# Attention scores: the low-key products of two PSUM banks on 64 rows each, ahead of the full-row products

## What is computed

```
def mla_attend(q_n, q_r, k_n, k_r, v):
    s = jnp.einsum('bqhd,bkhd->bhqk', q_n, k_n) + jnp.einsum('bqhr,bkr->bhqk', q_r, k_r)
    p = jax.nn.softmax(s.astype(jnp.float32) * MLA_SCALE, axis=-1)
    return jnp.einsum('bhqk,bkhd->bqhd', p.astype(v.dtype), v)
...
    qn_l, qr_l = q_side(s_lat)
    qr_l = apply_rope(qr_l, cos[:, None, :], sin[:, None, :])
    kn_all = jnp.concatenate([kn_c, kn_l], axis=1)
    kr_all = jnp.concatenate([kr_c, kr_l], axis=1)
```

## Time and profile before

| | |
|---|---|
| median of 3 runs | 3030.64 us (3027.17 to 3031.13) |
| the profiled execution's own time | 3030.1 us |
| its span in the trace | 3028.3 us |
| TensorE busy, of the span | 2884.8 us (95%) |
| VectorE, ScalarE, GpSimd busy | 51%, 39%, 8% |
| granted TensorE clock, mean | 0.978 of 2.4 GHz |

### The profile page before, as it was taken

One profiled execution on the slowest core, in us unless ns is written; L12 is line 12 of the kernel. 1 busy time (PEld: TensorE's weight loads), 2 busy tenths in 40 slices (PEclk: granted clock), 3 DMA queues, 4 the chain that ended last, 5 costly groups with the idle time before them and its releaser, 6 DMA issues. The chain is left out here.

```text
span 3028.3 us, 38367 instructions
## 1 busy us (share of the span) xinstructions
PE 2884.8 (95%) x15527; PEld 2468.4 (82%) x15527; DVE 1531.3 (51%) x2792; ACT 1190.3 (39%) x1980; POOL 249.6 (8%) x291
## 2 busy tenths in 40 slices
PE   6999999999999999979979997999999999999798
PEld 4788888888888888868867886888888888887587
DVE  6536543554355535543333224666666666665444
ACT  5323312331233123332234213666666666665400
POOL 2100000000000000001220000202102022020000
PEclk9899999999999999989989998999999999999899
DMA  6301131113111311153341321001000101000522
GB/s 190 104 23 53 44 109 31 52 44 108 31 52 44 111 31 50 34 211 119 119 146 39 98 91 39 29 25 32 26 25 26 36 18 33 29 22 18 191 84 84
DMA packets 220177, 200.77 MB, mean 66 GB/s; under 512 B 12037, under 2 KB 190613, under 8 KB 220002
## 3 DMA queue, kind: packets, MB, share of 16 engines
q1 hardware_dynamic: 204946, 176.52, 19.0%
q0 software_dynamic: 4656, 16.56, 1.4%
q10 hardware_dynamic: 10400, 5.24, 0.6%
HBM read 157.34 MB, written 40.95 MB: 65 GB/s over the span
## 5 line engine op out<-in xcount | busy, mean ns | idle before, releaser
L40 PE MATMUL e_pj<-e_u_hi,e_w_hi 128*128 128x512 f32 (+1 forms) x864 | 309.5, 358 | 1.0 <-PEq L57 1.0
L40 PE MATMUL e_pj<-e_u_hi,v_w_hi 128*128 128x512 f32 (+1 forms) x864 | 309.1, 358 | 0.0
L41 PE MATMUL e_pj<-e_u_lo,e_w_hi 128*128 128x512 f32 (+1 forms) x864 | 307.5, 356 | 0.0
L42 PE MATMUL e_pj<-e_u_hi,e_w_lo 128*128 128x512 f32 (+1 forms) x864 | 307.3, 356 | 0.0
L41 PE MATMUL e_pj<-e_u_lo,v_w_hi 128*128 128x512 f32 (+1 forms) x864 | 307.0, 355 | 0.0
L42 PE MATMUL e_pj<-e_u_hi,v_w_lo 128*128 128x512 f32 (+1 forms) x864 | 306.8, 355 | 0.0
L1939 ACT CAST t_pt_hi<-t_ring 128x512 fp32r<-128x512 f32 (+1 forms) x384 | 181.5, 519 | 237.0 <-PE t_ring L2123 237.0
L40 PE MATMUL o_y_bank<-o_w_hi,o_m_hi 128*128 128x512 f32 x576 | 228.1, 396 | 32.8 <-DVE o_w_lo L1313 29.0
L2024 DVE TENSOR_TENSOR t_pt_lo<-t_ring,t_pt_hi 128x512 fp32r<-128x512 f32 (+1 forms) x384 | 216.1, 598 | 52.3 <-ACT t_pt_hi L1939 50.8
L41 PE MATMUL o_y_bank<-o_w_lo,o_m_hi 128*128 128x512 f32 x576 | 226.6, 393 | 0.0
L42 PE MATMUL o_y_bank<-o_w_hi,o_m_lo 128*128 128x512 f32 x576 | 226.5, 393 | 0.0
(11 more groups left out here) (398 smaller groups left out, 6387.6 us busy)
## 6 DMA issues: line engine op xcount, KB each, us to landing
e_w_raw<-in_ev_w_in SPq DMA_DIRECT2D x72, 512.0 KB, 4.7
v_mw<-in_mod_w SPq DMA_DIRECT2D x32, 512.0 KB, 3.8
l_w_raw<-in_od_w_in SPq DMA_DIRECT2D x21, 512.0 KB, 4.0
o_m_raw<-mixT SPq DMA_DIRECT2D x20, 512.0 KB, 5.4
o_w_raw<-in_ev_w_out SPq DMA_DIRECT2D x16, 512.0 KB, 9.6
zgT<-l_lat_q POOLq DMA_DIRECT2D x16, 512.0 KB, 3.6
t_zg<-zgT SPq DMA_DIRECT2D x32, 256.0 KB, 2.7
ogT<-t_zg SPq DMA_DIRECT2D x32, 256.0 KB, 2.0
```

The lines of the kernel that those rows point to most:

```text
L40: nc.tensor.matmul(out, whi, xhi, start=first, stop=False)
L41: nc.tensor.matmul(out, whi, xlo, start=False, stop=False)
L42: return nc.tensor.matmul(out, wlo, xhi, start=False, stop=last)
```

## The change

For banks 1 and 0, the product with the low part of the key is made first, before anything else of the tile, and from the high part of the query alone: a matmul on 64 rows, bank 1 on rows 64 to 127, bank 0 on rows 0 to 63 (`hi_rows`). The high query is needed on both halves, so GpSimd copies it to the other half of a new buffer `qx` (`other_half`), once per head. Low query·low key is thereby left out for these two banks. Bank 2 keeps its five full matmuls; banks 1 and 0 have four full ones left. The number of matmuls stays at 15 per tile.

Space for `qx` comes from three places: `zg` has one buffer instead of two, `part` lies in `w_raw`, and so the first weight load of each pair of heads waits for the rotation that uses it (`turn_ok`).

```
+        qx = s.sb("qx", [P, LAT], F32R)
...
-        zg = [s.sb(f"zg{x}", [P, 512]) for x in range(2)]
-        turn, part = s.sb("turn", [P, LAT]), s.sb("part", [P, 512])
+        zg = s.sb("zg", [P, 512])
+        turn, part = s.sb("turn", [P, LAT]), w_raw[:, 0:512]
...
                 if n > 4:
                     sp.wait_ge(w_ok, n - 1)
+                    if (kind, h % 2) == ("k", 0):
+                        sp.wait_ge(turn_ok, h)
...
             def store(h, x):
                 sp.wait_ge(ring_free, at[("PV", h, x)])
-                sp.dma_start(og_dst[h * P:h * P + P, 512 * x:512 * x + 512], zg[x][:, :]).then_inc(og_out[x], 16)
-                if h + 1 < AH:
-                    sp.wait_ge(og_out[x], 16 * (h + 1))
-                    gates(h + 1, x)
+                sp.dma_start(og_dst[h * P:h * P + P, 512 * x:512 * x + 512], zg[:, :]).then_inc(og_out, 16)
+                if (h, x) != (AH - 1, 1):
+                    sp.wait_ge(og_out, 16 * (2 * h + x + 1))
+                    gates(h + x, 1 - x)
...
+            def other_half(h):
+                r = DR * (h % 2)
+                o = DR - r
+                pool.wait_ge(qs_hi_ok, h + 1)
+                pool.tensor_copy(qx[o:o + DR, :], f(qs[h % 2][r:r + DR, :])).then_inc(qx_ok, 1)
+
             add(0, 0)
             add(0, 1)
+            other_half(0)
             for h, t in slots:
                 for op in projections(h, t):
                     if op[0] == "qr":
                         add(op[1], op[2])
+                if t == 5 and h + 1 < AH:
+                    other_half(h + 1)
...
+                hi_rows = [slice(DR * g, DR * g + DR) for g in range(2)]
+                high = [(qs[b] if g == b else qx)[hi_rows[g], tok] for g in range(2)]
+                if t == 0:
+                    pe.wait_ge(qx_ok, h + 1)
+                for j in (1, 0):
+                    k0, n = KEYS[j]
+                    nc.tensor.matmul(S[:, k0:k0 + n], high[j], kr2[1][hi_rows[j], k0:k0 + n], start=True, stop=False)
                 for j in SCORE_ORDER:
                     k0, n = KEYS[j]
                     out = S[:, k0:k0 + n]
-                    mm3(nc, out, (qn[b][0][:, tok], qn[b][1][:, tok]), (kn[b][0][:, k0:k0 + n], kn[b][1][:, k0:k0 + n]), True, False)
-                    nc.tensor.matmul(out, qs[b][:, tok], kr2[0][:, k0:k0 + n], start=False, stop=False)
-                    last = nc.tensor.matmul(out, qs[b][:, tok], kr2[1][:, k0:k0 + n], start=False, stop=True)
+                    mm3(nc, out, (qn[b][0][:, tok], qn[b][1][:, tok]), (kn[b][0][:, k0:k0 + n], kn[b][1][:, k0:k0 + n]), j == 2, False)
+                    last = nc.tensor.matmul(out, qs[b][:, tok], kr2[0][:, k0:k0 + n], start=False, stop=j != 2)
+                    if j == 2:
+                        nc.tensor.matmul(out, qs[b][:, tok], kr2[1][:, k0:k0 + n], start=False, stop=True)
                     if j == 1:
                         last.then_inc(qk_part, 1)
                 last.then_inc(qk_done, 1)
```

More of the change, by code:

```diff
@@ L1801, in stage_attend @@
             "qk_part", "qk_done", "most_ok", "bias_ok", "exp_ok", "rec_ok", "prob_ok"))
-        rope_part, rope_own = s.sem("rope_part"), s.sem("rope_own")
+        rope_part, rope_own, qx_ok = s.sem("rope_part"), s.sem("rope_own"), s.sem("qx_ok")
         turn_ok, qs_hi_ok, qs_ok = s.sem("turn_ok"), s.sem("qs_hi_ok"), s.sem("qs_ok")
-        zg_in, og_out = [s.sem(f"zg_in{x}") for x in range(2)], [s.sem(f"og_out{x}") for x in range(2)]
+        zg_in, og_out = s.sem("zg_in"), s.sem("og_out")
         wq_src = a["od_w_uq"].rearrange("a (k p) n -> p (a k) n", p=P)
@@ L1859, in gates @@
             def gates(h, x):
-                sp.dma_start(zg[x][:, :], zg_src[h * P:h * P + P, 512 * x:512 * x + 512]).then_inc(zg_in[x], 16)
+                sp.dma_start(zg[:, :], zg_src[h * P:h * P + P, 512 * x:512 * x + 512]).then_inc(zg_in, 16)
             def store(h, x):
                 sp.wait_ge(ring_free, at[("PV", h, x)])
-                sp.dma_start(og_dst[h * P:h * P + P, 512 * x:512 * x + 512], zg[x][:, :]).then_inc(og_out[x], 16)
-                if h + 1 < AH:
-                    sp.wait_ge(og_out[x], 16 * (h + 1))
-                    gates(h + 1, x)
+                sp.dma_start(og_dst[h * P:h * P + P, 512 * x:512 * x + 512], zg[:, :]).then_inc(og_out, 16)
+                if (h, x) != (AH - 1, 1):
+                    sp.wait_ge(og_out, 16 * (2 * h + x + 1))
+                    gates(h + x, 1 - x)
             for kind, h in LOADS[:4]:
@@ L1871, in _ @@
             gates(0, 0)
-            gates(0, 1)
             for h, t in slots:
@@ L1881, in _ @@
             store(AH - 1, 1)
-            for x in range(2):
-                sp.wait_ge(og_out[x], 16 * AH)
+            sp.wait_ge(og_out, 16 * 2 * AH)
         @block.gpsimd
@@ L2014, in low @@
                     dve.wait_ge(ring_done, at[op])
-                    dve.wait_ge(zg_in[x], 16 * (h + 1))
-                    nc.vector.scalar_tensor_tensor(zg[x][:, :], ps[:, :], 0.5, zg[x][:, :], ALU.mult, ALU.mult).then_inc(ring_free, frees(op))
+                    dve.wait_ge(zg_in, 16 * (2 * h + x + 1))
+                    nc.vector.scalar_tensor_tensor(zg[:, :], ps[:, :], 0.5, zg[:, :], ALU.mult, ALU.mult).then_inc(ring_free, frees(op))
                 else:
```

## The result

The changed kernel takes 3046.82 us in the median of 6 runs (3040.72 to 3050.77), the kernel before, run beside it, 3032.16 (3027.17 to 3034.62). The ratio is 1.0049, with a 95% interval of 1.0039 to 1.0059: 15 us slower, 12 to 18. A second comparison gave 1.0044 (1.0031 to 1.0058). The direction and the range were right; the forecast of 32 us of loss was more than twice what came.

A forecast was written before the change was run, and what follows sets the result against it. TensorE was taken to bound 106 of 128 tiles: 106 x 0.27 = 28.6 us lost, plus 2.2 in the 22 others and 1.4 for the first head, 32 us in all, giving 3063 us, range 3042 to 3083.

The forecast's parts named there:

- TensorE is the limit in 106 tiles, 22 wait: Of 128 attention tiles, 21 wait for the exponential and the first for `t_qs`; in the other 106 TensorE is the limit.
- Emptying the array before the pair, 0.09: On TensorE, going from 128 to 64 rows ahead of the two passes loses 0.09 us per tile.
- The first load open, 0.105: The weight load of the first 64-row pass is no longer hidden under the matmul before it: 0.105 us per tile.
- The pass until the array is empty, 0.32: The second 64-row pass takes its listed 0.39 minus 0.07, so 0.32 us per tile, until the array is empty.
- The load behind, 0.105: The weight load for bank 2's first matmul, after the 64-row pair, lies open again: 0.105 us per tile.
- The load of the second, 0.105: The second 64-row pass's weight load runs behind the first load, so that pass starts 0.105 us after the first.
- a rival, with 0.165 per tile and 3050 us: Weight loads of the two halves run at once, 0.165 us lost per tile, 19 us in all, 3050 us; chance 0.17.
- The waiting tiles, 2.2 us: In the 22 tiles where the array idles before the scores, 0.1 us each comes through, 2.2 us in all.
- The first wait, 1.4 us: For the first head, the GpSimd copy, taken as 2.6 us, delays the first scores by 1.4 us once.
- Nothing for the gates, the weights and the other copies: Shared `zg`, the weight load waiting for `turn_ok`, and the copies for 15 of 16 heads are covered and cost nothing.
- The other side: Rival: the 64-row pair costs no emptying, loads stay hidden, both passes stream at once; 27 us less, 3004 us; chance 0.10.

The follow-up runs named there:

- same-half kernel: The changed kernel with both 64-row products on the same half of the rows, the one holding the head's own high part: 3070.96 us, ratio 1.0129 to the kernel before.
- full-row kernel: The changed kernel with the two early low-key products on all 128 rows, everything else kept: 3029.70 us beside 3031.50 for the kernel before, ratio 1.0.
- first shared stay: Kernel before's transposes as 64-row pairs, followed directly by the 64-row score pair, in tiles 2 and 6; full rows elsewhere: 3026.66 us beside 3031.35, ratio 0.9985.
- kernel with late pairs in tiles 3 and 4: Shared 64-row transposes and score pairs in tiles 2 and 6, plus, in even heads' tiles 3 and 4, the pair last in the scores: 3023.55 us, ratio 0.9973.

## Why the prediction was right and wrong

- **TensorE is the limit in 106 tiles, 22 wait:** nearly. The waits are the same 21 and 1. But in tile 5 of seven odd heads TensorE waits too, 0.12 us, and the pair costs nothing there: it is 99 tiles.
- **Emptying the array before the pair, 0.09:** 0.09. **The first load open, 0.105:** 0.11. **The pass until the array is empty, 0.32:** 0.43 - 0.11 = 0.32. **The load behind, 0.105:** 0.10.
- **The load of the second, 0.105 ("I let it run behind the first load"):** this is the step that failed. It measured 0.00. I took it from two consecutive loads on the same rows, which the same-half kernel confirms for the same half (0.11), but loads of different halves start together. It is 106 x 0.105 = 11 us of the 32. I had this case as a rival, with 0.165 per tile and 3050 us; it measured 0.16 and 3047. The Trainium skill (TensorEngine Tiling (Array Packing), Key Properties) says that different tiles load and multiply in parallel, and the trace agrees.
- **The waiting tiles, 2.2 us:** wrong; they cost nothing, and against the full-row kernel their waits take up 1.6 us (below). One reason is the same: bank 1 comes 0.1 less late.
- **The first wait, 1.4 us:** the wait is 7.1 where it was 6.1, 1.0 us. The copy takes 2.1 us, between my bounds of 1.3 and 2.6:

```profile
1856.72 1.22 DVE L2040 SCALAR_TENSOR_TENSOR t_qs<-t_turn,t_qs 64x1024 fp32r<-64x1024 f32 x1 [1.74 <-ACT t_qs L1955]
1856.75 2.08 POOL L1909 CAST t_qx<-t_qs 64x1024 fp32r<-64x1024 f32 x1 [1.15 <-ACT t_qs L1955]
```

- **Nothing for the gates, the weights and the other copies:** held, by the full-row kernel.
- **The other side,** no emptying at all: wrong, and the reason I gave against it (the same 0.07 before the listed end, whatever the operation) held for a float32r product too.

With the measured terms the prediction's sum would be 106 x 0.16 + 1.0 = 18 us, more than came. The traces of the full-row and the changed kernel place the rest. I take for each tile the time from the last matmul ahead of its scores to its fifteenth scores matmul, less the same time with full rows. In the 99 tiles it is 0.157 on average (0.12 to 0.19), together 15.6 us. In the seven tiles 5 it is -0.04 each, -0.3. In the 22 waiting tiles it is -1.6: their waits shorten by more than the pair costs. The sum is 13.7, beside the 13.6 between first and last scores (956.6 - 943.0), and with the 1.0 of the first wait 14.7 us, as measured. So of the 32 us forecast, 17.5 didn't come: 11 for the load of the second in the 99 tiles, 2.2 for the seven tiles, 3.8 for the waiting ones, 0.4 for the copy.

## What to carry to other kernels

Price a change of row count as a fixed fee for going in and out (here 0.09 us each way and a weight load open behind each, 0.39 in all for float32r products), and compare it with what the overlap of one stay saves: one 512-column pass, 0.228 us, is too little, and the same pair gains 0.165 in each tile where it joins a stay that another use has paid for. When a price has to come from the nearest row, ask whether the row shares the property that the change introduces: two loads one after the other on the same rows said nothing about loads on different ones. And measure what a pass is worth in both directions: adding one cost its full length here, removing two gave three quarters. Last, a list of waits leaves out the short ones: where the next step starts late by 0.1 us, TensorE isn't the limit, and seven tiles were counted wrongly by that.

## What the runs showed that was not expected

- Weight loads of the two row halves start together and take as long as one (0.18 listed); in one half they follow each other at 0.11.
- Float32 transposes and float32r products on 64 rows follow each other without an emptying.
- In head 15, where TensorE waits 1.3 to 2.4 us ahead of five tiles, the granted clock fell to its lower level for 3.4 us in six traces and not in the others. In the first shared stay that made tile (15, 1) 12.2 us long, where it is 10.6 in the kernel with late pairs in tiles 3 and 4: as much as the differences compared at the end.
- Transposes of 64x128 pieces in two halves go at 0.06 us a pair, where a 128x128 one takes 0.11, so in tile (2, 3) eight of them repay the two changes of rows with 0.08 us over. That gave no shorter kernel by itself.
